# A gather ring of seven slots instead of eight, and the whole output projection kept in SBUF

## The reference

```python
q = (hf @ wq).reshape(T, PEER_HEADS, 2, PEER_DKEY // 2)
scores = jnp.einsum('thjd,hjkd->thjk', q, subkeys)
...                                     # top 16 of each side, then top 16 of the sums
act = gelu(einsum('td,tkd->tk', xt, u_tab[et]))
out = einsum('tk,tkd->td', gt * act, v_tab[et])
```

## Time and profile before

| what | value |
|---|---|
| median of 3 runs | 3229.7 us |
| span of the profiled execution | 3239.0 us |
| busy share: TensorE, VectorE, ScalarE, GpSimd | 73%, 72%, 47%, 35% |
| bytes moved by DMA | 1310.00 MB, 404 GB/s over the span |
| gathers | 1024 of 1 MiB |
| first gather issued | 225.4 us |

### The profile page before, as it was taken

The page is one execution under the profiler, slowest core; times in us unless marked ns, Lnnn a source line. Parts: engine busy times, 40 slices in busy tenths (PEclk is TensorE's granted clock), DMA queues, the critical chain, the costliest instruction groups (busy, mean ns, idle before and its releaser), DMA issues.

```text
span 3239.0 us, 45251 instructions
## 1 busy us (share of the span) xinstructions
PE 2362.4 (73%) x15268; PEld 1189.2 (37%) x15268; DVE 2336.7 (72%) x6331; ACT 1515.7 (47%) x4895; POOL 1143.2 (35%) x1029
## 2 busy tenths in 40 slices
PE   7786678677785777757687678867687677875555
PEld 5372334333452434514243333524344243441111
DVE  6478856878668778677767776677766877688554
ACT  2225454455544455454544545445553545545443
POOL 0004333333333333333443333334333334434442
PEclk7787979878987889978898887978888799888777
DMA  9859999999999999999999999999999999999997
GB/s 365 359 204 420 413 420 409 419 416 420 415 415 415 408 418 398 415 419 418 419 412 418 409 417 420 415 410 411 418 409 418 408 419 420 393 417 414 422 421 323
DMA packets 204830, 1310.00 MB, mean 404 GB/s; under 512 B 26333, under 2 KB 41869, under 8 KB 52278
## 3 DMA queue, kind: packets, MB, share of 16 engines
q0 software_dynamic: 147456, 1073.81, 80.4%
q1 hardware_dynamic: 56422, 232.65, 18.1%
q10 hardware_dynamic: 720, 0.66, 0.1%
HBM read 1302.15 MB, written 7.16 MB: 404 GB/s over the span
## 4 chain that ended last, share of the span: by engine, by line
DMA 41%; PE 27%; DVE 14%; ACT 7%; issue 4%; POOL 3%; SPq 0%; ACTq 0%; DVEq 0%; POOLq 0%
DMA ringbuf<-in_p_uv,IDX 37%; PE PS L1053 14%; DVE ringbuf L1953 8%; PE PS L973 3%; PE PS L1012 3%; POOL ringbuf L674 3%; PE PS L816 2%; ACT v_th L1415 2%; DMA WB<-in_p_wi 2%; ACT v_w L1424 2%; ACT DIAG L1431 2%; PE PS L747 1%; DMA WB<-in_p_ada 1%; ACT v_sq L1412 1%; PE PS L893 1%
## 5 line engine op out<-in xcount | busy, mean ns | idle before, releaser
L674 POOL DMA_INDIRECT ringbuf<-in_p_uv,IDX x1024 | 1142.8, 1116 | 2067.6 <-PE PS L1053 1670.9
L1053 PE MATMUL PS<-ringbuf,DIAG 64*64 64x512 f32 x8192 | 1271.4, 747 | 740.6 <-ACT DIAG L1431 722.0
L1953 DVE SCALAR_TENSOR_TENSOR ringbuf<-ringbuf,H 128x1024 f32<-128x1024 f32 x1024 | 1240.4, 1222 | 592.0 <-DMA ringbuf<-in_p_uv,IDX 587.3
L1053 PEld LDWEIGHTS PS<-ringbuf,DIAG 64*64 64x64 f32 x8192 | 308.2, 155 | 1415.5 <-ACT DIAG L1431 964.2
L1412 ACT ACTIVATE v_sq<-v_y 128x2 f32<-128x2 f32 x512 | 104.4, 204 | 1337.7 <-DVE ringbuf L1953 1337.7
L1415 ACT ACTIVATE v_th<-v_sq,v_y 128x1 f32<-128x1 f32 x1024 | 340.5, 379 | 17.1
L1424 ACT ACTIVATE v_w<-v_th,v_g 128x1 f32<-128x1 f32 x800 | 266.1, 379 | 37.3
L1012 PEld LDWEIGHTS PS<-HT,WB 128*128 128x128 f32 x1888 | 232.0, 204 | 72.5 <-issue 56.9
L1012 PE MATMUL PS<-HT,WB 128*128 128x128 f32 x1888 | 243.1, 290 | 7.0 <-DMA WB<-in_p_wq 6.1
L1431 ACT ACTIVATE DIAG<-fold,v_w 128x64 f32<-128x64 f32 x800 | 234.7, 340 | 13.0
L816 PE MATMUL PS<-WB,HT 128*128 128x256 f32 (+2 forms) x816 | 182.3, 380 | 39.4 <-DMA WB<-in_p_wi 39.4
(11 more groups left out here) (327 smaller groups left out, 2531.4 us busy)
## 6 DMA issues: line engine op xcount, KB each, us to landing
WB<-in_p_wq SPq DMA_DIRECT2D x59, 1024.0 KB, 12.1
WB<-in_p_wi SPq DMA_DIRECT2D x37, 1024.0 KB, 9.4
ringbuf<-in_p_ahead SPq DMA_DIRECT2D x20, 1024.0 KB, 8.0
WB<-in_p_ada SPq DMA_DIRECT2D x16, 1024.0 KB, 15.2
ringbuf<-in_p_uv,IDX POOLq DMA_INDIRECT x1024, 12.6
WF<-in_p_ada SPq DMA_DIRECT2D x12, 1024.0 KB, 12.0
WB<-in_p_wi SPq DMA_DIRECT2D x14, 768.0 KB, 9.3
WB<-in_p_wo SPq DMA_DIRECT2D x8, 1024.0 KB, 14.2
```

The costliest lines, as they stand in the source:

```text
L674: pool.indirect_dma_start(out=ring[n % RING], out_offset=None, in_=table, in_offset=bass.IndirectOffsetOnAxis(ap=IDX[:, k % 2, s:s + 1], a ...
L1053: mm = pe.matmul(PS[half:half + HALF, 2 * c + r, :], DIAG[r * HALF:(r + 1) * HALF, (n + q) % DIAGS, :], row[r * HALF:(r + 1) * HALF, D + c ...
L1953: dve.scalar_tensor_tensor(row, row, GELU_T, H2[:, k % 2, :], ALU.mult, ALU.mult, accum_out=Y[:, b, q:q + 1]).then_inc(dotted, 1)
```

## The change

`RING` goes from 8 to 7 and `KEPT` from 3 to 4. The slot's 8 KB a partition go to `KEEP`, so the whole output projection is resident for a layer, and kind `wo` no longer occurs in the order of chunks. The ahead chunks get three slots instead of four (ring slots 0 to 2, with `WF` over slots 3 to 6), and their issues move in SP's order so that the waits fit.

```diff
-RING = 8
-KEPT = 3
+RING = 7
+KEPT = 4
...
-AHEAD_SLOTS = 4
+AHEAD_SLOTS = 3
...
             for i in range(8):
                 chunk(("wi", 0, i))
-                if i == 1:
-                    chunks_ahead(1)
-            chunks_ahead(2)
+            chunks_ahead(3)
             sp.wait_ge(bias_stored, 16)
...
                 if j == 0:
                     sp.wait_ge(skew_in, 16)
-                    chunks_ahead(2)
+                    chunks_ahead(1)
...
                         if i == 3:
                             chunks_ahead(4)
+                        if i == 5:
+                            chunks_ahead(1)
                         if i >= 4:
                             keys(0, i - 2)
```

## The result

The changed kernel takes 3304.5 us (median of 4 runs, 3297.52 to 3327.39) against 3230.2 us before: the ratio is 1.0238, with a 95% interval of 1.0217 to 1.0259, which is 77 us slower (70 to 84). The forecast was 3285 us, +55.

A forecast was written before the change was run, and what follows sets the result against it. The prediction took the kernel to be bound by bytes, with the slot loop just fast enough to keep a gather queued. Bytes -15, loop +60 and start +10 made +55 us: 3229.7 + 55 = 3285 us, range 3236 to 3332.

The forecast's parts named there:

- The loop: Gather ring with seven slots: gathers issued later leave holes in the DMA engines' work; +60 us, bounds 20 to 95.
- three pair times: Ring: a pair's second row has 14.9 us instead of four pair times, 19.9, leaving 7.9 us for its gather.
- the floor: Gathers: least time from issue to landing, taken as 6.5 us, the fastest of all 1024.
- the limit: Gathers: a landing time below 6.5 + 3.7 = 10.2 us becomes a hole as long as the shortfall.
- the same sum over the 148 stretches: Stretches of 20 us, 250 to 3210 us: each one's shortfall against 10.2 us counted once, 72 us in all.
- The bytes: Output projection's fourth chunk: six loads less, 6.29 MB, all on the path; -15 us, 0 as the other bound.
- The start: Ahead chunks through three slots: up-projection 5 us and routing 11 us later, first gather at 241; +10 us, bounds +4 to +16.
- The marks named for the profile: Profile after: 1303.7 MB, queue shares near 96.5%, heavy stretches 0.85 to 0.95, median landing 10, VectorE waits some 60 us more.
- rival 2: Gather loop: floor about 1 us lower, limit 9.1 us, loop costs 20 us; sum +15, 3245 us; chance 0.2.
- The slot not missed: Ring: bytes decide, only saved bytes and the start remain; -15 + 4 = -11 us, 3219 us; chance 0.09.
- The lower floor: Gather loop: same as rival 2, floor about 1 us lower, loop costs 20 us, 3245 us; chance 0.2.
- The loop that loses more than once a stretch: Ring: shortfall lost at each heavy pair, 144 us if twice a stretch; sum +139, 3369 us; chance 0.1.

The follow-up runs named there:

- ring8_wait7: Kernel before with all eight buffers, but GpSimd waits before gather n for the sum of row n-7, as with seven slots: 3290.1 us, ratio 1.0188.
- start3_alone: Kernel before with eight slots and old weights; only the ahead chunks pass through three slots in the changed SP order: 3248.4 us, ratio 1.0054.
- weights_alone: Kernel before without the 8 loads of the output projection's fourth chunk; its matmuls read the third resident chunk: 3222.0 us, ratio 0.9972.
- ring7_alone: Kernel before with seven ring slots and nothing else changed; the eighth slot's space stays a buffer for ahead chunks: 3287.0 us, ratio 1.0175.
- ring6_alone: Kernel before with six ring slots and nothing else changed; two spare buffers keep the start as before: 3515.0 us, ratio 1.0876.
- ring7_short: ring7_alone with ScalarE's tanh of each pair left out, which shortens each row's loop by some 0.75 us: 3247.4 us, ratio 1.0060.
- ring8_short: Kernel before with eight slots and ScalarE's tanh of each pair left out: 3231.8 us, ratio 1.0000.
- after_hold: Changed kernel, but from the second tile on the second query chunk loads only after the output projection's fourth part is used: 3298.7 us, ratio 1.0200.

## Why the prediction was right, and where not

**The loop: the mechanism right, the size, +60 against +56 measured, by luck.** That a second row is left with three pair times, that this is too little in the heavy places, and that the cost depends on the moment of the issue (ring8_wait7) and steeply on the loop's length all held. In the quiet end it was not quite "just enough": 409 GB/s against 421. And the floor was too high. The fastest landing in the traces of start3_alone and weights_alone is 5.7 us, below the 6.5 of the earlier trace rows; with seven and with six slots it is lower still (ring7_alone, then ring6_alone):

```profile
DMA to landing us min/median/max: 5.7/12.6/24.1
```

```profile
DMA to landing us min/median/max: 5.6/10.5/20.0
```

```profile
DMA to landing us min/median/max: 5.4/9.0/17.0
```

With a floor of 5.6 us the limit is 9.3 us and the same sum over the 148 stretches gives 26 us, half of the 56. The same holds for the other two tests: 0.75 us off a limit of 9.3 takes 16 us from that sum, where ring7_short gave 37 back, and for six slots (5.6 + 5.0 us) it gives 103 against 283. So the losses come about twice a stretch with seven slots, and nearer three times with six, as far as this estimate goes; no run counts them one by one. A floor taken too high and losses counted too rarely cancelled each other. The Trainium skill's estimate of the floor, 5.4 us as an estimate from "DMA: Bandwidth & Descriptors" (the anatomy of one DMA), is nearer to these 5.4 to 5.7 us than my 6.5; its sum of 20 us was as wrong all the same, because of the counting.

**The bytes: wrong, -15 against nothing measured.** 77 - 56 - 17 = +4 us is left for this term, give or take some 10, if the three parts add up. This is most of what the forecast of +55 lacks to the +77; the rest is the start. The step that failed is the sentence that the first two query chunks no longer queue behind the fourth chunk's use, "which I cost at nothing". I asked whether TensorE would miss them where they were; I didn't ask whether the queue would. With the old place given back the term is -8 in the changed kernel (65 - 73, as uncertain as the +4) and -17 of 20 us with eight slots. The bound that I had set, 0 "if the freed time falls where the queue is empty anyway", was the case that came.

**The start: the places right, the size too small, +10 against +17.** The last chunk landed at 219.2 in the changed kernel, not at 223, as SP had come to it at 212.04 already. VectorE had waited 10.8 us for it and began routing at 222.3 and not at 226, 7.5 us later than before (11 were worked out). The up-projection's matmuls waited 5.8 us and began at 85.4, 4.4 us later (5 were taken):

```profile
219.24 3.11 DVE L1584 SCALAR_TENSOR_TENSOR XM<-ringbuf,CBC,XM 128x512 f32<-128x512 f32 x4 [10.78 <-DMA ringbuf<-in_p_ahead]
...
85.41 2.08 PE L846 MATMUL PS<-WF,CT 128*128 128x512 f32 x2 [5.80 <-DMA WF<-in_p_uk]
```

So the first gather went at 232.9 and not at 241. Of the 4.4 us about half arrives later: in start3_alone the output projection starts at 181.5 against 179.3 before. The forecast also hid 6 of the first gather's 16 us behind the query matmuls; start3_alone hid none of its 9.8 (3249.3 - 3239.0 = 10.3).

**Why 17 and not 10: the profiled start was a slow one.** I took the 9.3 us between the profiled span and the median as that execution's spread and carried them over. On spans the forecast of 3294 met 3295.7, but that was luck: the profiled execution of the changed kernel was its fastest of four, that of before slower than its other runs. A part of that spread lies in the start. Of the kernels with the start of before, the traces show the first gather at 225.4 us where TensorE's mean granted clock from 100 to 200 us was 0.74 (ring8_short, also 0.74: 225.2), at 219.2 to 222.1 where it was 0.77 or 0.78 (ring7_alone, ring8_wait7 and three more), and at 215.6 where it was 0.84 (weights_alone). With the three-slot start it is 240.8 at 0.71 (after_hold), 235.2 at 0.76 (start3_alone) and 232.9 at 0.83 (the change). The rows from 100 to 200 us of before and of weights_alone:

```profile
100.00:200.00 100.00, 78.07 (x438) 44.45 (x438) 48.72 (x116) 26.37 (x84) 0.00 (x0) 0.74 0.73 293
```

```profile
100.00:200.00 100.00, 75.95 (x486) 47.46 (x487) 56.96 (x127) 26.70 (x87) 0.00 (x0) 0.84 0.73 291
```

So both starts are longer where TensorE is slow, and the profile of before had caught a slow one. Compared at a like clock the new start puts the first gather off by 13 to 16 us (0.76 against 0.77 and 0.78) and by 17 us (0.83 against 0.84), which is near the +17 of the medians; 10 us came from 0.76 against 0.74. This rests on one trace of each kernel, and no kernel was made to test it.

**The marks named for the profile.** The bytes (1303.7 MB) and VectorE's waits (+67 us; some 60 were given) came as said. The queues' shares add up to 97.5%, not 96.5, and of the 148 stretches of 20 us from 250 us on only 6 stand under 0.95, the lowest at 0.87 (before: 2 and 0.92). That was the wrong mark: the share hides most of the holes, the GB/s show them (415 before and 405 after on the mean from 250 to 3200 us). The changed kernel's trace has no landing times of the gathers, but ring7_alone's has: the median is 10.5, as foreseen, and the least 5.6, which by the mark itself speaks for rival 2.

**The rivals.** The slot not missed is out (ring7_alone). The lower floor was right as a floor and wrong as a price, +20. The loop that loses more than once a stretch was given 0.1 and +144; its count of twice a stretch fits, on the lower floor's shortfalls.

## What to carry to other kernels

Before a slot is taken from a ring, ask what it is worth in time to the tightest row: with rows handled in pairs, going from eight slots to seven took 3.7 of the 4.97 us of a pair from the second row of each. In a kernel bound by bytes, a load saved counts only where the queue stays full without it, so look at which other loads move with it, and what is queued in the places where the compute loop is longest; here a load that came "earlier, for free" took back about half of the gain or more. And before a term is read from one profiled execution, find out how that execution differs from the others: here its clock in the start was worth up to 10 us.

## What the runs showed of the hardware

The busy share of the DMA engines stays near 1 while they lose time: 1.00 at 409 GB/s against 1.01 at 421 in the quiet end, and even six slots show 0.94 at 346 GB/s. Where the traffic is the same, the GB/s column is the one to read.

A gather of 1 MiB, from the start of GpSimd's instruction to the landing, took 5.4 us at the least (ring6_alone) and 12.6 us at the median with eight slots; the fewer the slots, the shorter the median (10.5 with seven, 9.0 with six), while the kernel gets slower.
